# Reading a rare-path flag earlier, loading an activation table earlier, and reordering the sums of a mixture-of-experts scatter

## What is computed

```
x = x + g1 * o                                   # after the mixers
h = modulate(rmsnorm(x, n2), sh2, sc2)
g_sel = argmax(h @ w_rg + b_rg)                  # one of 4 groups
hid = silu(h @ w_gate) * (h @ w_up)
y = (hid * combine) @ w_down                     # two of the group's four experts
x = x + g2 * y
# next layer, or the end: y = x * rsqrt(mean(x * x) + EPS) * g
```

## Time and profile before

| | |
|---|---|
| median of three executions | 870.04 us |
| the profiled execution, its own time | 866.05 us |
| its span, first to last instruction | 864.1 us |
| mean granted TensorE clock | 0.972 of 2.4 GHz |
| TensorE matmul busy | 790.5 us (91%) |
| VectorE busy | 545.6 us (63%) |
| ScalarE busy | 450.0 us (52%) |
| GpSimd busy | 42.1 us (5%) |
| scatter matmuls | L735, 128, 334 ns median |
| activation table loads | 13 of 1283 ns, two at L1442 |

### The profile page before, as it was taken

How to read it: one execution, slowest core, us unless ns; L and a number is a source line. 1 busy time by engine, 2 the same in 40 slices (tenths; PEclk the granted TensorE clock), 3 DMA queues, 4 the chain that set the end, 5 groups by cost and what they waited for, 6 DMA issues and landing times. The chain is left out here.

```text
span 864.1 us, 10375 instructions
## 1 busy us (share of the span) xinstructions
PE 790.5 (91%) x3836; PEld 549.6 (64%) x3836; DVE 545.6 (63%) x916; ACT 450.0 (52%) x752; POOL 42.1 (5%) x36
## 2 busy tenths in 40 slices
PE   5999999788989999999889999978898899999984
PEld 2664644345956888888756564434595578888874
DVE  4136441785459889989540835077554688999965
ACT  3015742455336777777340376046543577777742
POOL 0002510000000000000000142000000000000000
PEclk9999999999999999999999999986998899999998
DMA  9951008856437799999733100754641069999901
GB/s 369 362 218 74 25 0 328 306 185 246 154 146 290 266 371 369 359 378 365 269 116 106 36 25 1 291 184 158 218 174 48 0 220 372 378 359 376 360 28 76
DMA packets 35083, 185.92 MB, mean 215 GB/s; under 512 B 5200, under 2 KB 6352, under 8 KB 19536
## 3 DMA queue, kind: packets, MB, share of 16 engines
q1 hardware_dynamic: 31760, 184.11, 56.7%
q10 hardware_dynamic: 3264, 1.05, 0.5%
HBM read 182.53 MB, written 2.62 MB: 214 GB/s over the span
## 5 line engine op out<-in xcount | busy, mean ns | idle before, releaser
L1622 DVE TENSOR_TENSOR split<-ring,split 128x2048 fp32r<-128x2048 f32 x96 | 219.9, 2290 | 27.7 <-ACT split L1232 25.1
L1232 ACT CAST split<-ring 128x2048 fp32r<-128x2048 f32 x96 | 183.4, 1910 | 18.5 <-PE psum L715 14.5
L686 PE MATMUL psum<-split,y_hi 128*128 128x512 f32 x512 | 162.7, 399 | 0.0
L686 PEld LDWEIGHTS psum<-split,y_hi 128*128 128x128 f32 x512 | 93.7, 188 | 19.6
L686 PE MATMUL psum<-split,y_lo 128*128 128x512 f32 x256 | 100.6, 393 | 0.0
L790 PE MATMUL psum<-ring,hT 128*128 128x512 f32 x192 | 84.1, 593 | 0.1
L715 PE MATMUL psum<-split,hidT 128*128 128x512 f32 x256 | 70.3, 396 | 1.8 <-DVE hidT_lo L1627 1.8
L769 PE MATMUL psum<-hT,ring 128*128 128x384 f32 x192 | 69.2, 499 | 0.0
L790 PEld LDWEIGHTS psum<-ring,hT 128*128 128x128 f32 x192 | 36.1, 190 | 43.2 <-issue 41.6
L715 PEld LDWEIGHTS psum<-split,hidT 128*128 128x128 f32 x256 | 47.4, 188 | 14.5 <-DVE hidT_lo L1627 3.6
L686 PEld LDWEIGHTS psum<-split,y_lo 128*128 128x128 f32 x256 | 48.0, 188 | 11.1
(11 more groups left out here) (248 smaller groups left out, 1233.3 us busy)
## 6 DMA issues: line engine op xcount, KB each, us to landing
ring<-in_w_gu SPq DMA_DIRECT2D x64, 1024.0 KB, 5.2
ring<-in_w_ada SPq DMA_DIRECT2D x40, 1024.0 KB, 5.1
ring<-in_w_down SPq DMA_DIRECT2D x32, 1024.0 KB, 5.0
ring<-in_w_in SPq DMA_DIRECT2D x16, 768.0 KB, 4.8
ring<-in_first SPq DMA_DIRECT2D x8, 1024.0 KB, 12.6
ring<-in_w_out SPq DMA_DIRECT2D x8, 1024.0 KB, 4.9
ring<-in_w_in SPq DMA_DIRECT2D x8, 784.0 KB, 6.1
par<-in_par SPq DMA_DIRECT2D x1, 1632.0 KB, 11.3
```

The lines of the kernel that those rows point to most:

```text
L686: last = pe.matmul(dst, x[:, g, t, :], w[:, j, :], start=(t == 0 and i == 0), stop=(t == KD - 1 and i == 2))
L1232: act.copy(splits[n % SPLITS][:, 0, :], slot(key)).then_inc(raised("whi", l, p), 1)
L1622: tt(lo, slot(unit_key(l, p, n)), hi.bitcast(F32), ALU.subtract).then_inc(raised("wlo", l, p), 1)
```

## The change

A step `flag` is put behind the `ahead` pieces of each layer. TensorE and ScalarE wait for the flag and read it there; the branch stays in `more`. VectorE skips the new step and still reads the flag in `more`, as SyncE does behind its last load. ScalarE loads the Ln and Exp table at the start of the scatter step, ahead of the squares, and the load in `more` moves inside the branch. In the scatter, TensorE waits for the last group's halves only where it first uses them, and the sum of a chunk goes group by group, high and low part together.

```diff
-    s += [("router",), ("hrow", 0), ("rank",), ("hrow", 1), ("hrow", 2), ("h_lo",)] + ahead[3:]
+    s += [("router",), ("hrow", 0), ("rank",), ("hrow", 1), ("hrow", 2), ("h_lo",)] + ahead[3:] + [("flag",)]
...
                     for g in range(NG):
                         pe.wait_ge(*taken(("selT", l, p, g)))
-                        for half in range(2):
-                            pe.wait_ge(*taken(("yg", l, p, g, half)))
+                        if g < NG - 1:
+                            for half in range(2):
+                                pe.wait_ge(*taken(("yg", l, p, g, half)))
                     for c in range(KD):
                         pe.wait_ge(*fill(("sc", l, p, c)))
                         dst = bank(("sc", l, p, c))
-                        for i, src in enumerate((y_hi, y_lo)):
-                            for g in range(NG):
+                        for g in range(NG):
+                            if g == NG - 1 and c % 4 == 0:
+                                pe.wait_ge(*taken(("yg", l, p, g, c // 4)))
+                            for i, src in enumerate((y_hi, y_lo)):
                                 last = pe.matmul(dst[:, 0:TOK], src[:, g, c * P:(c + 1) * P], selT[:, g, :],
                                                  start=(i == 0 and g == 0), stop=(i == 1 and g == NG - 1))
...
-                    elif kind == "more":
+                    elif kind == "flag":
 
                         pe.wait_ge(sig["flag"], l + 1)
                         over = pe.value_load(flag[0:1, l:l + 1], min_val=0, max_val=1)
+                    elif kind == "more":
                         with pe.If(over != 0):
...
                 elif kind == "scatter" and not arg[0]:
+                    act.preload_act_table_set("natural_log_exp_and_others")
                     squares(l + 1, 0)
...
-                    elif kind == "more":
+                    elif kind == "flag":
 
                         act.wait_ge(sig["flag"], l + 1)
                         over = act.value_load(flag[0:1, l:l + 1], min_val=0, max_val=1)
+                    elif kind == "more":
                         with act.If(over != 0):
...
-                        act.preload_act_table_set("natural_log_exp_and_others")
+                            act.preload_act_table_set("natural_log_exp_and_others")
...
+                    if kind == "flag":
+                        continue
```

## The result

The changed kernel takes 862.48 us (median of four executions, 860.9 to 863.24) where the kernel before, run beside it, takes 870.06 (four, 869.57 to 870.13): ratio 0.9906, 95% interval 0.9886 to 0.9926. A ratio here is estimated over all executions of both kernels and isn't the quotient of the two medians. Faster both times, and by less than 2%; by how much is a question to which the experiments come back.

A forecast was written before the change was run, and what follows sets the result against it. ScalarE, last to arrive at each layer's end, and TensorE's idle time before the scatter were taken to lie on the path. Terms 3.2 + 2.6 + 1.2 = 7.0 us took 870.04 to 863.0 us, range 860.2 to 866.0.

The forecast's parts named there:

- Scatter order: Scatter at each layer's end: TensorE no longer idles 1.60 us for the last half's low part; 3.2 us in all.
- Table load: ScalarE's load ahead of Ln moves to the scatter's start, hidden before the first square; 1.28 us a layer, 2.6 in all.
- Read leaves: ScalarE's idle 2.85 us before Ln loses the flag read, taken as 0.6 us a layer; 1.2 in all, ends 0 and 3.0.
- rival 1: ScalarE's stall before Ln is the jump alone, the read takes no measurable time: 864.2 us, chance 0.18.
- ScalarE's idle time about 2.3 us: Sign that the forecast is right: ScalarE idles about 2.3 us between last square and Ln, not 2.85.
- The room of 1.5 us between square and packet: Layer 1's end: the read fits between last square's start (851.33) and code packet (852.83), at most 1.5 us, branch and request included.
- The packet near 852.1: Instruction-queue packet at layer 1's end, taken as fitting VectorE, whose last work was said to end 0.57 us earlier.
- Read arrives: The read's new place behind the `ahead` pieces: covered by waiting time in both layers; cost 0, ends 0 and 0.5 us.
- Late next: After the gains ScalarE resumes at 852.5, TensorE's sums nearly tie at 852.4; VectorE's late read stays covered by 1.1 us.
- Half of it at the end of layer 0, where it passes through layer 1: Half of the 7.0 us gain falls at layer 0's end and makes layer 1 start earlier, some 3.5 us.
- The median lies 3.99 us above that execution, and I carry it unchanged: The gap from profiled execution to median was kept: 859.1 us forecast for the profiled execution, 863.0 for the median.
- Rival 2: ScalarE's stall before Ln goes whole with the early read, Ln waits only for the last sum: 860.2 us, chance 0.08.

The follow-up runs named there:

- e10: Kernel before with only the new scatter, plus 8 never executed TensorE instructions in layer 0's skipped block: 865.47 us, ratio 0.9969 to before.
- e8: e2 with ScalarE's jump taken ahead of the squares, which stand in both branches: 856.75 us, ratio 0.9857 to the kernel before.
- e7: Kernel before with only the table load moved to the start of the scatter step: 865.63 us, ratio 0.9953 to before.
- e6: e2 with TensorE's and ScalarE's flag reads put back behind the scatter: 861.1 us, ratio 0.9902 to the kernel before.
- e2: Changed kernel plus 8 never executed TensorE instructions in layer 0's skipped block: 859.07 us, ratio 0.9918 to the kernel before.
- e3: Kernel before with only the new scatter (order and waits): 867.89 us, ratio 1.0005 to before.
- e4: Kernel before with 252 more never executed TensorE instructions in layer 0's skipped block: 868.29 us, ratio 1.0028 to before.
- e5: Changed kernel, unchanged, timed again: 864.21 us, ratio 0.9948 to the kernel before.

## Why the prediction was right, and where it was wrong

The time was right: 863.0 forecast, 862.48 measured, inside the likeliest case's own range. That it came so close is luck in part, as the last two steps show. Step by step:

- **Scatter order, 2 x 1.60:** right. No idle time ahead of it in either layer; 1.80 and 1.66 us won once the stop is gone (e10 against the earlier trace rows).
- **Table load, 2 x 1.28:** right, and hidden where the forecast put it. The drain of the Trainium skill (ScalarE: Activation LUTs, What ACT_TABLE_LOAD costs) isn't seen: Ln follows the last sum of e8 within 0.04 us with the load beside other work, and the earlier trace rows has the load at its bare length. Nor is e7's idle time any shorter without the load. e7's interval in time doesn't exclude a larger gain.
- **Read leaves, 2 x 0.6:** somewhat too large. In layer 1's profile it is 2.85 - 2.62 = 0.23 us, and 0.23 by e6 against e2; in layer 0 e6 against e2 gives 0.64. That is 0.87 in all for 1.2, between rival 1 (the stall is the jump alone, 864.2) and the forecast. Most of the stall is the jump, as rival 1 had it. "ScalarE's idle time about 2.3 us" failed at 2.62. The room of 1.5 us between square and packet was mostly the branch and its request, not the read. The packet near 852.1, said to come 0.57 us after VectorE's last work, comes 0.8 after it (851.29).
- **Read arrives, 0:** right. The cast in layer 0 idles 0.81 us for its weights against 0.98, so the read went into waiting time.
- **Late next:** VectorE's late read is not the wait, not even in e8. The near tie of ScalarE and TensorE did not come up, for a reason that the prediction had put at nothing: TensorE's own early read. Its sums were reckoned to be over 852.4 - 837.58 = 14.8 us after the last expert at the latest and were over after 13.5, since its wait fell from 1.34 to 0.22 us. With both reads late that wait is 1.32 (e6), with both early and all else the same 0.56 (e2). ScalarE, forecast to resume at 14.9, did so at 15.06.
- **"Half of it at the end of layer 0, where it passes through layer 1":** this step failed. TensorE's jump was costed at nothing new ("that fetch stays, since the jump stays"); in fact the stream ahead of its target got three instructions shorter, and the jump then cost 2.81 us more and a stretch of half clock. Together they cost 3.6 us (21.29 against e2's 17.68), all that this layer had won.
- **"The median lies 3.99 us above that execution, and I carry it unchanged":** failed too, the other way. After's profiled execution, 863.24, stands at the top of its own four, not 4 us below them. It was forecast at 859.1 and came 4.1 us later, of which 3.6 are the stop that wasn't foreseen; the median was forecast 3.99 above it and lies 0.76 below. The two errors nearly cancel, and so 863.0 came out.

How large is the change, then? By the ratio over the four executions each of the result 8.2 us (6.4 to 9.9); by 12 and 23 executions 4.5 us (ratio 0.9948, 2.5 to 6.5). The forecast's steps without the stall give 7.0; with it the 3.6 us of layer 0 go and 3.4 stay. The larger sample fits the second and excludes the first; the small one does the reverse, but its four executions of before all stand in the upper part of the range that this kernel shows elsewhere, and both profiles of after have the stall. So the smaller gain is the likelier one, and it isn't settled. e2, where only the stop is taken away, gives 0.9918: 7.1 us of 866.58 (5.0 to 9.2), and its timeline 3.56 + 3.24 = 6.8. The sum of the steps was about right for e2, and the kernel after is that one less a stall.

**Rival 2** (the stall goes whole, Ln right behind the sums, 860.2) didn't happen by reading early. e8 shows that it takes the jump itself to be moved, and then it does happen.

## What to carry to other kernels

Here a rare-path flag cost 0.2 to 0.6 us to read and some 2.6 us to jump over: move the branch beside other work, not only the read. When instructions are added or taken ahead of a long skipped block, look at where the engine lands; two passes of one operation with 2.8 us of "issue" between them were a landing just ahead of a code page's end here, and eight instructions of padding in the block mended it. And four executions of a kernel that scatters by 1% can't price a change of half of that: time more of them, and read terms off the timeline.

## What the runs showed of the hardware that was not expected

- Landing near a page's end stops TensorE 2.80 to 2.90 us (after, e3, e4, e5), at shifts of -3 and +252 instructions and not at 0, +5 or +128. The next page's packet starts only 0.5 us after TensorE resumes, lands at 2.1, and the stopped pass starts 1.2 to 1.4 us after that.
- ScalarE's jump over the block costs 2.45 to 2.73 us of idle time with the flag long in a register; a read of the flag from SBUF costs 0.23 to 0.64 us alone and 0.36 to 0.41 each in a row of four. Beside the table load and the wait for the first chunk (e8) the same jump delays the first square by 0.6 us.
- The clock falls to 0.50 behind such a stop, and in some executions of one and the same program for 3.4 us at the start of layer 1 and again near 540 us, each worth at most 1.7 us (an estimate). What triggers it in one execution and not in the next is open.
